# Six modulation blocks: matrix products on TensorE replaced by scaled chunk sums on GpSimd and VectorE

## The reference, cut to what matters

```python
mod   = jax.nn.silu(c)     @ w_ada + b_ada     # c: (1, 1024), w_ada: (1024, 6144)
mod_c = jax.nn.silu(c_ctx) @ w_ada + b_ada
```

## Time and profile before

| | |
|---|---|
| median of 3 runs | 1448.44 us |
| the profiled execution | 1447.1 us, its span 1445.3 us |
| TensorE busy | 1394.3 us, 96% of the span |
| VectorE, ScalarE, GpSimd busy | 606.4, 432.9, 59.3 us |
| chain of work that ended last | PE 88%, DMA 5%, DVE 4%, ACT 2% |
| granted TensorE clock, mean | 0.999 |

### The profile page before, as it was taken

How to read it: one execution, slowest core, us unless ns; L and a number is a source line. 1 busy time by engine, 2 the same in 40 slices (tenths; PEclk the granted TensorE clock), 3 DMA queues, 4 the chain that set the end, 5 groups by cost and what they waited for, 6 DMA issues and landing times.

```text
span 1445.3 us, 15985 instructions
## 1 busy us (share of the span) xinstructions
PE 1394.3 (96%) x6460; PEld 857.3 (59%) x6460; DVE 606.4 (42%) x1090; ACT 432.9 (30%) x742; POOL 59.3 (4%) x113
## 2 busy tenths in 40 slices
PE   6999999899999999999999999999999999999998
PEld 5777775576433333333333476655458888888886
DVE  5225556745434334334443464467143222224224
ACT  4225765623100110010200263456143222223222
POOL 0000110000210000001000001000000000000000
PEclk9999999999999999999999999999999999999999
DMA  9541117628899999999999922200023213213001
GB/s 354 221 158 59 58 59 317 236 70 337 323 424 423 425 422 424 427 424 425 422 423 427 322 101 107 117 1 0 0 99 135 106 69 117 102 73 117 30 1 59
DMA packets 32371, 304.07 MB, mean 210 GB/s; under 512 B 6315, under 2 KB 6315, under 8 KB 10536
## 3 DMA queue, kind: packets, MB, share of 16 engines
q1 hardware_dynamic: 29592, 298.69, 51.2%
q0 software_dynamic: 2272, 3.52, 0.7%
q10 hardware_dynamic: 432, 0.81, 0.2%
HBM read 302.59 MB, written 4.25 MB: 212 GB/s over the span
## 4 chain that ended last, share of the span: by engine, by line
PE 88%; DMA 5%; DVE 4%; ACT 2%; issue 1%; DVEq 0%; SPq 0%; POOL 0%; ACTq 0%
PE ps L58 83%; DMA ring<-in_w 5%; PE ps L1279 2%; PE ps L1007 1%; PE ps L963 1%; DVE TMP L2135 1%; DMA X<-in_x 0%; PE ps L674 0%; PE ps L694 0%; PE ps L876 0%; PE ps L922 0%; DVE TMP L2138 0%; DVE B L2198 0%; DVE B L1998 0%; DVE UL L1919 0%
## 5 line engine op out<-in xcount | busy, mean ns | idle before, releaser
L58 PE MATMUL ps<-ring,B 128*64 128x512 f32 (+2 forms) x688 | 175.1, 589 | 3.7 <-DVE B L2198 2.5
L58 PE MATMUL ps<-XH,WH 128*128 128x512 f32 (+1 forms) x368 | 140.9, 383 | 1.3 <-DVE XL L1919 0.7
L58 PE MATMUL ps<-XL,WH 128*128 128x512 f32 (+1 forms) x368 | 139.8, 380 | 0.0
L58 PE MATMUL ps<-XH,WL 128*128 128x512 f32 (+1 forms) x368 | 139.7, 380 | 0.0
L58 PEld LDWEIGHTS ps<-ring,B 128*64 128x64 f32 (+1 forms) x688 | 55.7, 142 | 93.8 <-issue 88.1
L58 PE MATMUL ps<-B 128*64 128x512 f32 (+5 forms) x408 | 110.0, 554 | 0.3 <-DMA B<-in_w 0.3
L1622 ACT ACTIVATE TMP<-ps 64x512 f32<-64x512 f32 x32 | 19.0, 595 | 303.7 <-PE ps L58 303.0
L2254 DVE TENSOR_TENSOR X<-ps,X 128x512 f32<-128x512 f32 x112 | 72.2, 687 | 63.6 <-PE ps L58 63.6
L1919 DVE TENSOR_TENSOR WL<-ring,WH 128x2048 fp32r<-128x2048 f32 x25 | 57.3, 2293 | 73.7 <-ACT WH L1813 73.7
L1813 ACT ACTIVATE WH<-ring 128x2048 fp32r<-128x2048 f32 x25 | 47.9, 1917 | 124.6 <-PE ps L58 124.6
L58 PE MATMUL ps<-ring,TMP 128*64 128x512 f32 x336 | 75.2, 594 | 4.1 <-DMA ring<-in_w 4.1
(11 more groups left out here) (352 smaller groups left out, 2302.5 us busy)
## 6 DMA issues: line engine op xcount, KB each, us to landing
ring<-in_w SPq DMA_DIRECT2D x57, 2048.0 KB, 24.9
B<-in_w SPq DMA_DIRECT2D x21, 2048.0 KB, 26.8
ring<-in_w_ada SPq DMA_DIRECT2D x12, 2048.0 KB, 8.6
MORE<-in_w SPq DMA_DIRECT2D x11, 2048.0 KB
ring<-in_w_gu SPq DMA_DIRECT2D x8, 2048.0 KB, 8.2
TO<-in_w SPq DMA_DIRECT2D x7, 2048.0 KB, 17.3
ring<-in_w_in SPq DMA_DIRECT2D x6, 2048.0 KB, 12.2
ring<-in_w_down SPq DMA_DIRECT2D x4, 2048.0 KB, 7.3
```

Of the source, the lines that this page charges most:

```text
L58: return e.matmul(o, l, r, start=first, stop=last, skip_group_check=True)
```

## The change

In blocks 0 to 5 the sum over the eight chunks of a block is no longer made by TensorE. For a coefficient vector and a block, the 8 chunks are each multiplied by that chunk's coefficient (one scalar for each partition) and added elementwise into an accumulator of 128 x 512; TensorE then only adds over the 128 partitions, by a matmul with ones. There are ten such accumulators: both vectors for blocks 0 to 3, and c alone for blocks 4 and 5.

- GpSimd makes the accumulators of c for blocks 0 to 3: per block one scaling, and 7 times a scaling into a scratch tile and an addition. Each of the 60 operations waits for the one before it.
- VectorE makes those of c_ctx for blocks 0 to 3 and those of c for blocks 4 and 5: per block one scaling and 7 multiply-adds, four operations in each of the iterations 2 to 13.
- TensorE makes three sums, after units 6, 10 and 14 (`SUM_AT`), of 4, 4 and 2 vectors, side by side on the four strips of P[7]. Sum 0 waits for 30 operations of GpSimd, sum 1 for 60. Each is copied, turned in the next unit, and added to the bias, as before.
- The accumulators lie in MORE, a tile that is otherwise first used for an expert's weights in a later stage. GpSimd's scratch is LW.
- A slot with a block is now used up when GpSimd and VectorE have both finished with it.
- Some semaphores are merged, and counts that others wait for are renumbered. Blocks 6 to 11 are computed as before.

```diff
+    SUM_AT = {6: 0, 10: 1, 14: 2}
...
+    AC = [MORE[:, 512 * v:512 * v + 512] for v in range(8)]
...
     def consumed(j):
         if j in ada_of:
-            return ada_mm, ada_of[j] + 1
+            b = ada_of[j]
+            return (ac_pool, 15 * b + 15) if b < 4 else (ac_dve, 8 * b + 8) if b < 6 else (ada_mm, b - 2)
...
         for i in range(4, I_ADA[8]):
             e.wait_ge(*consumed(before[i]))
+            if ada_of.get(before[i], 6) < 4:
+                e.wait_ge(ac_dve, 8 * ada_of[before[i]] + 8)
             load(i)
...
+        e.wait_ge(cs_set, 4)
+        for b in range(4):
+            w, d = slot(I_ADA[b], 8, 512), AC[2 * b]
+            e.wait_ge(slot_in[where[I_ADA[b]]], landed[I_ADA[b]])
+            e.tensor_scalar(d, w[:, 0, :], CS[:, 0, 0:1], None, ALU.mult).then_inc(ac_pool, 1)
+            for c in range(1, 8):
+                e.wait_ge(ac_pool, 15 * b + 2 * c - 1)
+                e.tensor_scalar(LW[:, 0:512], w[:, c, :], CS[:, c, 0:1], None, ALU.mult).then_inc(ac_pool, 1)
+                e.wait_ge(ac_pool, 15 * b + 2 * c)
+                e.tensor_tensor(d, d, LW[:, 0:512], ALU.add).then_inc(ac_pool, 1)
...
+        def ada_sum(g):
+            e.wait_ge(ac_pool, (30, 60, 60)[g])
+            e.wait_ge(ac_dve, (16, 32, 48)[g])
+            if g:
+                e.wait_ge(ada_mod, g)
+            else:
+                e.wait_ge(brow_cp, 2)
+            for v in range(4 if g < 2 else 2):
+                m = mm(e, P[7][32 * v:32 * v + 32, :], ones[:, 0:32], AC[v if g != 1 else 4 + v], True, True)
+            m.then_inc(ada_mm, 1)
...
+                    if c == 5 and n - 1 in SUM_AT:
+                        sum_turn(SUM_AT[n - 1])
...
-            if n in ADA_AT:
-                ada_product(ADA_AT[n])
+            if n in SUM_AT:
+                ada_sum(SUM_AT[n])
...
+        def ada_part(b, cs):
+            w, d, r = slot(I_ADA[b], 8, 512), AC[2 * b + 1 if b < 4 else b - 4], 1 if b < 4 else 0
+            e.wait_ge(slot_in[where[I_ADA[b]]], landed[I_ADA[b]])
+            if b == 0:
+                e.wait_ge(cs_set, 4)
+            if b == 4:
+                e.wait_ge(ada_mm, 1)
+            for c in cs:
+                if c:
+                    e.wait_ge(ac_dve, 8 * b + c)
+                    e.scalar_tensor_tensor(out=d, in0=w[:, c, :], scalar=CS[:, c, r:r + 1], in1=d, op0=ALU.mult, op1=ALU.add).then_inc(ac_dve, 1)
+                else:
+                    e.tensor_scalar(d, w[:, 0, :], CS[:, 0, r:r + 1], None, ALU.mult).then_inc(ac_dve, 1)
...
         for n in range(16):
             proj_low(n + 1)
-            if n - 1 in ADA_AT:
-                ada_rows(ADA_AT[n - 1])
+            if n - 1 in SUM_AT:
+                sum_rows(SUM_AT[n - 1])
+            if 2 <= n < 14:
+                ada_part(n // 2 - 1, range(4 * (n % 2), 4 * (n % 2) + 4))
...
-            if n - 1 in ADA_AT:
-                ada_cols(ADA_AT[n - 1])
+            if n - 1 in SUM_AT:
+                sum_cols(SUM_AT[n - 1])
```

More of the change, by code:

```diff
@@ L183, in body @@
     ce = small[:, 0:16].rearrange("p (k r) -> p k r", r=2)
-    AD = [TMP[:, 2048 + 512 * g:2560 + 512 * g] for g in range(2)] + [B2[:, 2048 + 512 * g:2560 + 512 * g] for g in range(2)]
+    AC = [MORE[:, 512 * v:512 * v + 512] for v in range(8)]
+    AD = [TMP[:, 2048:2560], None] + [B2[:, 2048 + 512 * g:2560 + 512 * g] for g in range(2)]
     Z0 = small[:, 32:48]
@@ L419, in body @@
     wo_hi, wo_lo, wo_mm, x1 = (sem(n) for n in ("wo_hi", "wo_lo", "wo_mm", "x1"))
-    h2_sq, h2_rs, h2_T, h2c_act, h2c_dve, h2n, lg_mm, lg_cp, lg_T, rt_step, ms_set, rank_mm, s0_set = (
-        sem(n) for n in ("h2_sq", "h2_rs", "h2_T", "h2c_act", "h2c_dve", "h2n", "lg_mm", "lg_cp", "lg_T", "rt_step", "ms_set", "rank_mm", "s0_set"))
+    h2_sq, h2_rs, h2_T, h2c_act, h2c_dve, h2n, lg_mm, lg_cp, lg_T, rt_step, ms_set, rank_mm = (
+        sem(n) for n in ("h2_sq", "h2_rs", "h2_T", "h2c_act", "h2c_dve", "h2n", "lg_mm", "lg_cp", "lg_T", "rt_step", "ms_set", "rank_mm"))
     eg_sub, e2_sub, eg_exp, gate_set, si_set = (sem(n) for n in ("eg_sub", "e2_sub", "eg_exp", "gate_set", "si_set"))
@@ L424, in body @@
         sem(n) for n in ("oh_set", "ga_mm", "ga_xt", "up_mm", "up_sl", "up_hg", "hg_T", "ht_cp", "down_mm", "yh_set", "yl_set"))
-    tbl_out, tbl_in, idx_set, xn_out, xg_zero, row_set, cm_mm, cm_add = (
-        sem(n) for n in ("tbl_out", "tbl_in", "idx_set", "xn_out", "xg_zero", "row_set", "cm_mm", "cm_add"))
+    tbl_out, tbl_in, xn_out, xg_zero, row_set, cm_mm, cm_add = (
+        sem(n) for n in ("tbl_out", "tbl_in", "xn_out", "xg_zero", "row_set", "cm_mm", "cm_add"))
     xg_in, pair_set = sem("xg_in"), sem("pair_set")
@@ L676, in tensor, with sum_turn @@
                     t.then_inc(xT_mm, 1)
-        def ada_product(b):
[L679 to L684, removed]
+        def ada_sum(g):
[8 more added lines that the diff above has]
+            m.then_inc(ada_mm, 1)
+        def sum_turn(g):
+            e.wait_ge(ada_row, g + 1)
+            for j in range(4):
+                t = e.transpose(P[7][:, 128 * j:128 * j + 128], AD[0][:, 128 * j:128 * j + 128], ident)
+            t.then_inc(ada_T, 1)
+        def ada_product(b):
+            w, o = slot(I_ADA[b], 8, 512), P[5]
+            e.wait_ge(ada_mod, 2 * (b - 6) + (2 if b > 6 else 3))
             e.wait_ge(slot_in[where[I_ADA[b]]], landed[I_ADA[b]])
@@ L690, in ada_turn @@
         def ada_turn(b):
-            e.wait_ge(ada_row, b + 1)
-            o, d = P[7 if b < 6 else 5], AD[b % 2 + 2 * (b // 6)]
+            e.wait_ge(ada_row, b - 2)
+            o, d = P[5], AD[b % 2 + 2]
             for j in range(4):
@@ L730, in tensor @@
                         e.wait_ge(sv_out, 4)
-                    if k == 3 and n - 1 in ADA_AT:
-                        ada_turn(ADA_AT[n - 1])
+                    if k == 3 and n - 1 in SUM_AT:
+                        sum_turn(SUM_AT[n - 1])
                     for c in range(2):
@@ new lines, in sum_rows, with sum_cols @@
+        def sum_rows(g):
+            if g:
+                e.wait_ge(ada_T, g)
+            e.wait_ge(ada_mm, g + 1)
+            e.tensor_copy(AD[0], P[7]).then_inc(ada_row, 1)
+        def sum_cols(g):
+            sums = P[7].rearrange("p (j v x) -> p j v x", j=4, v=4)[:, :, :, 0]
+            bias = bada[:, 8 * g:8 * g + 8].rearrange("p (b j) -> p j b", b=2)
+            m = MOD[:, 8 * g:8 * g + 8, :].rearrange("p (b j) r -> p j b r", b=2)
+            e.wait_ge(ada_T, g + 1)
+            if g < 2:
+                e.tensor_tensor(m, sums.rearrange("p j (b r) -> p j b r", b=2), bc(bias, 2), ALU.add).then_inc(ada_mod, 1)
+            else:
+                e.tensor_tensor(m[:, :, :, 0], sums[:, :, 0:2], bias, ALU.add).then_inc(ada_mod, 1)
@@ L1944, in ada_rows @@
         def ada_rows(b):
[L1945 to L1948, removed]
+            if b >= 8:
+                e.wait_ge(ada_T, b - 4)
+            e.wait_ge(ada_mm, b - 2)
+            e.tensor_copy(AD[b % 2 + 2], P[5]).then_inc(ada_row, 1)
         def ada_cols(b):
             m = MOD[:, 4 * b:4 * b + 4, :]
-            e.wait_ge(ada_T, b + 1)
@@ L1953, in ada_cols @@
-            e.tensor_reduce(m, P[7 if b < 6 else 5].rearrange("p (j g r) -> p j r g", j=4, g=4)[:, :, 0:2, :], AX, ALU.add).then_inc(ada_mod, 1)
-            e.wait_ge(ada_mod, 2 * b + 1)
+            e.wait_ge(ada_T, b - 2)
+            e.tensor_reduce(m, P[5].rearrange("p (j g r) -> p j r g", j=4, g=4)[:, :, 0:2, :], AX, ALU.add).then_inc(ada_mod, 1)
+            e.wait_ge(ada_mod, 2 * (b - 6) + 4)
             e.tensor_tensor(m, m, bada[:, 4 * b:4 * b + 4].unsqueeze(2).to_broadcast([128, 4, 2]), ALU.add).then_inc(ada_mod, 1)
@@ L2175, in vector @@
         step(e.tensor_scalar(cond, rank, CAP - 0.5, 2.0 * NE * CAP, ALU.is_gt, ALU.mult))
-        e.tensor_tensor(S0, S0, cond, ALU.add).then_inc(s0_set, 1)
-        e.wait_ge(s0_set, 1)
+        step(e.tensor_tensor(S0, S0, cond, ALU.add))
         def one_hot(p):
```

13 lines of the change are left out of this document (6 added, 7 removed).

## The result

The changed kernel takes 1498.94 us (median of 4 runs, 1496.51 to 1499.96), the kernel before 1448.51 on the same chip: a ratio of 1.0357, interval 1.0344 to 1.0369. The direction was as forecast, the size was not: 1476 was forecast, with a range up to 1494. The profiled execution took 1496.51 us, span 1494.8, so the difference to explain is +49.4 us, where the sum had +27.7.

The account below looks back on a forecast made before the run. TensorE bounded the kernel before; now GpSimd's chain would hold it: operation 60 at 29.6 + 50.2 + 37.6 = 117.4, plus 30.4 gives 147.8 (+26.0). With 1.7 for the clock, +27.7: median 1476.1 us, range 1457 to 1494.

Parts of the forecast that it names:

- GpSimd's price of a scaling: First stage, GpSimd's 32 scalings of 512 columns: 0.57 us each, from rows of copies and selects.
- The addition: First stage, GpSimd's 28 additions: 1.14 us each, two reads at the copy's price, bounds 0.57 and 1.71.
- The gap between dependent operations: GpSimd's chain of 60: 0.05 us each, 3 us in all, spent while VectorE works, so counted at nothing.
- The strict turns: VectorE and GpSimd never run beside each other on SBUF; VectorE's operations add 37.6 us to GpSimd's chain before operation 60.
- After operation 60: TensorE's path from GpSimd's last operation through sums 1 and 2, units 11 to 15 and two turns: 30.4 us.
- the clock: After idling, TensorE runs 3.4 us at half speed, losing 1.7 us; counted once, after sum 1.
- the 2 us that units 4 to 6 were each to lose: First stage: VectorE's five operations with GpSimd's between them take 8.5 us a unit, so units 4 to 6 run late.
- TensorE's saving of 10.7 us: First stage: six blocks' products cost 15.6 us, three sums and turns 4.9; 10.7 saved if nothing is late.
- the subtraction's cover of 3.2 us: VectorE's subtraction of the low half, due within 5.44 us less ScalarE's 1.06, has 3.2 us to spare.
- I take the shift as carried to the end in full.: What TensorE loses or gains in the first stage moves the program's end by the same amount.
- the not-slower case B: Rival: multiply-adds run beside GpSimd; TensorE waits 2.2 us and keeps 8.5 of its saving: 1440 us; chance 0.11.
- A: Rival: turns hold, but GpSimd's addition costs one copy or three: +10.0 or +41.9, about 1460 and 1492; chance 0.18.

Follow-up runs that it names:

- the padded kernel: The changed kernel with 44 matmuls of eight columns put ahead of TensorE's waits for sums 0 and 1: 1491.09 us, ratio 1.0273 to the kernel before.
- the run with GpSimd alone: The changed kernel with VectorE's 32 operations on blocks 0 to 3 left out: 1493.6 us (2 runs).
- where VectorE was alone: The changed kernel with all 60 GpSimd operations left out, VectorE keeping its 48: 1444.92 us, ratio 0.9974 to the kernel before.
- the three-block kernel: The kernel before with only blocks 3, 4 and 5 done by vector, on VectorE, with one sum after unit 14: 1448.6 us, ratio 0.9998.
- the kernel without the stop: Blocks 3 to 5 on VectorE only, plus 24 small matmuls ahead of TensorE's waits for experts 30 and 31: 1441.13 us, ratio 0.9960 to before.

## Why the prediction was wrong

What TensorE waits for was forecast rightly: GpSimd's chain, ahead of sums 0 and 1. It was wrong in size by 21.7 us. Of these 14.9 are the end of operation 60, 1.0 the path from there to dv, 5.8 the loss behind the experts. Without that last loss (the padded kernel, 1491.09) the time lies inside the range of 1457 to 1494, but there too only because two large errors inside the 14.9 nearly cancel.

1. **The step that failed: GpSimd's price of a scaling, 0.57 us "for a scaling of 512 columns", from copies of 32 partitions and selects.** It takes 1.57 alone: 32 x 1.00 = +32.0 us. (Two selects take 0.54, so one takes 0.27 and not 0.25; the line through the two points gives 0.57 all the same.) The bounds given for the addition (0.57 to 1.71) would have held it; the scaling was given none, though no row of before showed one. GpSimd alone, 120.7 us by 29.45 + 32 x 1.57 + 28 x 1.27 + 60 x 0.09, would have been behind TensorE without any neighbour.
2. **The addition**, 1.14 with bounds, took 1.27: +3.6 us. This estimate was good.
3. **The gap between dependent operations**, 0.05 from an operation of VectorE to one of GpSimd, counted at nothing "while VectorE works". The rows have 0.07 there, not 0.05. Between two operations of GpSimd it is 0.09, and VectorE is mostly not in the way: +5.4 us.
4. **The strict turns: "each VectorE operation adds its whole time to GpSimd's chain", 37.6 us.** 11.6 came (7.7 of them in the run with GpSimd alone as well): -26.0 (what is left of the difference after points 1 to 3). Subtractions come near to turns for as long as they run beside a GpSimd operation (0.95 of 1.08, 0.71 of 0.85), multiply-adds do not. And eight of the ten subtractions took 1.21 to 1.27, where the prediction had them above 1.23 (the other two took 1.74 and 1.87). The chain of waits and VectorE's timeline of the kernel after, in the same stretch, and VectorE's four multiply-adds alone:

```profile
37.04 1.88 POOL MORE L608
39.01 1.89 POOL LW L606
40.98 1.53 POOL MORE L608
```
```profile
37.68 5.38 DVE L1984 SCALAR_TENSOR_TENSOR MORE<-ring,MISC,MORE 128x512 f32<-128x512 f32 x4
...
134.99 3.10 DVE L1984 SCALAR_TENSOR_TENSOR MORE<-ring,MISC,MORE 128x512 f32<-128x512 f32 x4
```

Between 37.04 and 42.51 GpSimd does two additions and a scaling, worth 1.26 + 1.26 + 1.57 and two gaps, 4.3 us alone; VectorE's four multiply-adds are worth 3.10 alone. Strict turns would need 7.4 us, with nothing of the subtraction that ended at 37.75 counted; both were done in 6.0 (37.04 to 43.06), and GpSimd had begun its next operation by then. The rows of before that showed turns were of 32 partitions and short copies, and were carried to operations of another kind. Points 1 and 4 are both large and opposite, and that they nearly cancel is luck: the total of 27.7 was nearer to the truth than its terms were.

5. **After operation 60**: 33.2 us to dv, where 30.4 and 1.7 for the clock were said. That is right but for the clock: the half-clock stretch behind sum 1 lasted 5.0 us, worth 2.5 and not 1.7. Right were also the two waits before sums 0 and 1, their place, and SP's loads behind GpSimd; their lengths followed GpSimd: 24.7 and 19.2 us for 14 and 18. Wrong were the 2 us that units 4 to 6 were each to lose: unit 6 ended at 57.0, not at 62.
6. **TensorE's saving of 10.7 us**: 8.0 where VectorE was alone. The order on VectorE's queue (the sk copy behind the multiply-adds) cost 2.0. The prediction looked at the subtraction's cover of 3.2 us and not at the other operation for which TensorE waits.
7. **"I take the shift as carried to the end in full."** It was (the stretch from dv to the first gather is 248.6 us in both kernels), and on top of it came 5.9 us from the branch, a term that the sum put at nothing and that no row of before could show.

Of the rivals, the not-slower case B needed both that at most 8.6 of the 37.6 us be charged, where 11.6 were, and GpSimd at 50.2 us of work, which was the failed step. A reached 1492 with the addition at three times a copy; the time was near, the cause another.

## What to carry to other kernels

An operation that an engine does nowhere in the trace needs bounds of its own, also when it looks simple: here one form of a product cost 1.57 us and another 1.04, and the operation without a bound made the largest error of the forecast. Work given to a side engine must be finished by the time its reader comes, so count its chain first with all gaps; here VectorE alone, with three of the six blocks, made a kernel that is 0.4% faster, where all six with GpSimd's help made one 3.6% slower. And when the end moves by more than the changed stage, compare the stages behind it one by one, and the granted clock in them: a gain or loss at a branch that moves with the length of the program can hide a change of half a per cent, or pass for one.

## What the hardware showed that was not expected

- GpSimd multiplies 128x512 fp32 by a coefficient per partition in 1.57 us as tensor and scalar, in 1.04 as tensor and broadcast tensor; the addition of two tensors takes 1.26. The Trainium skill's GPSIMD Engine Reference (section 4.1) calls operations with one input "roughly line-rate", and only those with two slower than VectorE's; here the scaling is 1.57 against 0.48. Its section 3.1, by which the estimate for the addition was 1.2 us (1.12 by a quarter of its 4497 ns), comes near to the 1.26 of the trace.
- How GpSimd and VectorE share: a subtraction of 1024 columns cost a scaling beside it 0.95 us and mostly lost nothing itself, but took 2.3 for 1.23 beside additions back to back; multiply-adds cost a GpSimd operation beside them about 0.3 and were themselves stretched from 0.78 to 1.35 us beside scalings and additions, to 1.72 beside additions alone. SBUF — State Buffer (section "SBUF: two separate sides") of the Trainium skill has an exclusive lock held for the whole instruction; the trace agrees that the two contend, but not that neither runs beside the other: 7.4 us of work in 6.0, and 18.0 in 14.2.
- At a branch that is taken around a body, TensorE stood for 4.4 to 4.8 us and then ran at half clock for another 3.0 to 5.9, in seven of the eleven kernels; small matmuls alone made it come and go. What in the program's length decides was not settled: no run moved the length by less than 40 instructions, and one of the 11 executions of the three-block kernel took 1439.15 us, the time of the kernel without the stop, so it may not be there in each execution. The profile names no engine that it waits for. One rival is untested: that TensorE waits there for its own instructions. The profile's instruction queue q8 has a read of 0.02 MB between 2 and 3 us behind the last matmul of the experts in all eleven kernels, with the stop and without, so this view alone settles nothing.
- At one place of the program (268 us in the kernel before) the granted clock falls to 0.50 for some 3.4 us in nine of the eleven profiled executions and stays at 1.00 in two, behind the same wait. It is worth 1.6 us, beside a gain of 6.2.
